# A float32 model kernel on one core: norm chain, convolution and expert routing reordered, and the tiles that a matmul holds placed 64 bytes off the tiles it streams

## What is computed

```
h = x * rsqrt(mean(x*x) + 1e-6) * w_norm        # rmsnorm over 2048
proj = h @ w_in                                  # 2048 x (2048..8192)
...mix proj by head...                           # 16 heads of 128, or recurrence
x = x + mixed @ w_out
```

```
y = b;  for i in range(4): y = y + xpad[:, i:i+s] * w[i]
r = sigmoid(y @ wa + ba);  i = sigmoid(y @ wx + bx)
```

## Time and profile before

| | |
|---|---|
| time, median of 3 runs | 3451.39 us (3450.22 to 3453.89) |
| the profiled execution | 3451.02 us, of which the span from first to last instruction is 3449.3 us |
| mean granted TensorE clock | 0.989 of full speed |
| TensorE matmuls (PE) | busy 3354.9 us, 97% of the span |
| VectorE (DVE) | busy 2239.6 us |
| ScalarE (ACT) | busy 1609.1 us |
| HBM read | 565.45 MB, 165 GB/s over the span |

### The profile page before, as it was taken

How to read it: one execution, slowest core, us unless ns; L and a number is a source line. 1 busy time by engine, 2 the same in 40 slices (tenths; PEclk the granted TensorE clock), 3 DMA queues, 4 the chain that set the end, 5 groups by cost and what they waited for, 6 DMA issues and landing times.

```text
span 3449.3 us, 64243 instructions
## 1 busy us (share of the span) xinstructions
PE 3354.9 (97%) x26164; PEld 3169.4 (92%) x26164; DVE 2239.6 (65%) x3581; ACT 1609.1 (47%) x2065; POOL 6.8 (0%) x27
## 2 busy tenths in 40 slices
PE   7999999999999899999999999999999999999998
PEld 7999998999999889999998999998899889998786
DVE  6767665545454555555546898775577657789855
ACT  4444454666664544545534444334433443344444
POOL 0000000000000000000000000000000000000000
PEclk9999999999999999999999999999999999999999
DMA  4444444444444345454444454445544554445454
GB/s 173 147 146 158 146 159 147 156 149 150 154 158 169 137 141 175 147 183 147 157 173 147 172 183 169 172 169 188 194 172 171 183 195 172 171 172 180 173 204 150
DMA packets 98921, 570.02 MB, mean 165 GB/s; under 512 B 9408, under 2 KB 30272, under 8 KB 31296
## 3 DMA queue, kind: packets, MB, share of 16 engines
q1 hardware_dynamic: 98752, 567.58, 46.2%
HBM read 565.45 MB, written 2.10 MB: 165 GB/s over the span
## 4 chain that ended last, share of the span: by engine, by line
PE 92%; DVE 3%; ACT 2%; issue 1%; DMA 1%; DVEq 1%; ACTq 0%; POOL 0%; POOLq 0%; SPq 0%
PE bank L477 21%; PE bank L478 21%; PE bank L479 20%; PE bank L938 7%; PE bank L936 7%; PE bank L937 7%; PE bank L860 1%; PE bank L604 1%; DVE oT L1377 1%; PE bank L548 1%; PE bank L790 1%; PE bank L795 1%; PE bank L499 1%; ACT wh L969 1%; PE bank L784 1%
## 5 line engine op out<-in xcount | busy, mean ns | idle before, releaser
L477 PE MATMUL bank<-hh,wh 128*128 128x256 f32 x5760 | 1661.6, 288 | 32.8 <-DVE hl L1382 27.9
L1362 DVE TENSOR_TENSOR wl<-raw,wh 128x1024 fp32r<-128x1024 f32 x1052 | 1254.1, 1221 | 604.0 <-ACT wh L969 597.5
L478 PE MATMUL bank<-hl,wh 128*128 128x256 f32 x5760 | 1627.5, 283 | 0.0
L479 PE MATMUL bank<-hh,wl 128*128 128x256 f32 x5760 | 1626.2, 282 | 0.0
L969 ACT ACTIVATE wh<-raw 128x1024 fp32r<-128x1024 f32 x1052 | 1051.1, 1049 | 339.0 <-DMA raw<-w_in_a 139.1
L477 PEld LDWEIGHTS bank<-hh,wh 128*128 128x128 f32 x5760 | 1108.0, 192 | 46.4 <-issue 37.1
L478 PEld LDWEIGHTS bank<-hl,wh 128*128 128x128 f32 x5760 | 1094.0, 190 | 8.2 <-issue 7.2
L479 PEld LDWEIGHTS bank<-hh,wl 128*128 128x128 f32 x5760 | 1088.3, 189 | 0.0
L936 PE MATMUL bank<-wh,ah 128*128 128x512 f32 x1024 | 402.1, 393 | 3.5 <-DVE al L1919 3.5
L938 PE MATMUL bank<-wl,ah 128*128 128x512 f32 x1024 | 401.9, 392 | 0.0
L937 PE MATMUL bank<-wh,al 128*128 128x512 f32 x1024 | 400.1, 391 | 0.0
(11 more groups left out here) (314 smaller groups left out, 2628.7 us busy)
## 6 DMA issues: line engine op xcount, KB each, us to landing
raw<-peer_u SPq DMA_DIRECT2D x128, 1024.0 KB, 4.8
raw<-peer_v SPq DMA_DIRECT2D x128, 1024.0 KB, 4.8
raw<-w_in_a SPq DMA_DIRECT2D x64, 1024.0 KB, 4.8
raw<-w_in_c SPq DMA_DIRECT2D x64, 1024.0 KB, 4.8
raw<-w_kv SPq DMA_DIRECT2D x32, 1024.0 KB, 4.8
raw<-w_in_b SPq DMA_DIRECT2D x32, 1024.0 KB, 4.8
raw<-w_out_a SPq DMA_DIRECT2D x16, 1024.0 KB, 4.8
raw<-w_out_b SPq DMA_DIRECT2D x16, 1024.0 KB, 4.9
```

The lines of the kernel that those rows point to most:

```text
L477: eng.matmul(out, h_[:, k, :], high[:, k, :], start=(k == 0), stop=False)
L478: eng.matmul(out, h_[:, k, :], low[:, k, :], start=False, stop=False)
L479: last = eng.matmul(out, low_rows(c, k), high[:, k, :], start=False, stop=(k == KC - 1))
L1362: eng.tensor_tensor(low_half_out(c, half), raw_half(c, half), high_half(c, half).bitcast(F32), ALU.subtract).then_inc(lo_ready, 1)
```

## The change

Five parts.

1. **Norm chain.** The last two out-projection columns are added and squared one by one, so that most is done before the last unit ends. A dummy `Sqrt` on a spare tile is put ahead, and `rstd` is made by one `Sqrt` and a VectorE reciprocal over 128x256. VectorE multiplies the norm weights into `oT` beforehand; the scaling is then one 128x512 product by `rstd` per pair. All eight scalings come first, then all eight low parts. ScalarE's copies for unit 2 of the next stage move behind the norm. The first two units of a stage are multiplied together (`two_products`): first all that needs only `hh`, four matmuls per chunk, then all that needs `hl`, two per chunk. At the kernel's start the norm is put ahead of the parameter arithmetic and the weight splits, and waits only for the constants that it uses; the first weight load comes in two halves.
2. **Convolution.** The low part of unit `u + 4` moves behind the convolution.
3. **Routing.** `ROUTE_UNITS` goes from 5 to 4; the softmax of both tiles is done together, its second half after the low part of U0's unit 29.
4. **Tail.** `Sqrt` and a 128x2 reciprocal in place of Ln and Exp, with the dummy `Sqrt` ahead; half of the last weighing moves into the wait.
5. **Placement.** `eps` and `qw` (4 bytes each, a row of 32) now stand ahead of `raw`, and `wh` directly behind `wl`. Byte addresses within a partition, and their rest by 128, of before and of the change:

The diff, cut to what the text speaks of:

```diff
-ROUTE_UNITS = 5
+ROUTE_UNITS = 4
...
+        eps = sb("eps", [P, 1])
+        qw = sb("qw", [P, 1])
         m = ExitStack()
         raw = sb_in(m, "raw", [P, RAW, KC * P])
         m.close()
         wl = sb("wl", [P, RAW, KC * P], F32R)
+        wh = [sb(f"wh{n}", [P, KC, P], F32R) for n in range(RAW)]
...
+            def two_products(c, outs, high, low, split):
+
+                for k in range(KC):
+                    if k % 2 == 0:
+                        eng.wait_ge(hh_ready, split + k // 2 + 1)
+                    for n in range(2):
+                        if k % FH == 0:
+                            eng.wait_ge(lo_ready, 2 * (c + n) + k // FH + 1)
+                        eng.matmul(outs[n], wh[(c + n) % RAW][:, k, :], high[:, k, :], start=(k == 0), stop=False)
+                        eng.matmul(outs[n], low_rows(c + n, k), high[:, k, :], start=False, stop=False)
+                for k in range(KC):
+                    if k % 2 == 0:
+                        eng.wait_ge(hl_ready, split + k // 2 + 1)
+                    for n in range(2):
+                        last = eng.matmul(outs[n], wh[(c + n) % RAW][:, k, :], low[:, k, :], start=False, stop=(k == KC - 1))
...
-            eng.wait_ge(consts_ready, 1)
+            eng.wait_ge(first_consts, 1)
             for g in range(KC // 2):
                 norm_sum("A", g)
...
+                eng.activation(spare[:, 0:1], eps[:, :], ACT.Sqrt)
                 eng.wait_ge(ss_done, 8 * (NORM_AT[name] + 1))
-                rsqrt(rstd[:, :], B[4][:, 0:T], 1.0 / D).then_inc(rstd_ready, 1)
+                eng.activation(rstd[:, :], B[4][:, 0:T], ACT.Sqrt, bias=eps[:, 0:1], scale=1.0 / D).then_inc(rstd_ready, 1)
...
+                eng.drain()
                 eng.wait_ge(rstd_ready, NORM_AT[name] + 1)
+                eng.reciprocal(rstd[:, :], rstd[:, :])
+                eng.drain()
+
+                def scale(n, g, weight):
+                    if n == 0:
+                        last = eng.tensor_tensor(oT[:, 2 * g:2 * g + 2, :], oT[:, 2 * g:2 * g + 2, :],
+                                                 rstd[:, :].unsqueeze(1).broadcast_to([P, 2, T]), ALU.mult)
...
+                    if n == 0 and name != "A":
+                        for g in range(KC // 2):
+                            scale(n, g, weight)
+                        for g in range(KC // 2):
+                            low(n, g, dst, high)
+                        low_part(0, NORM_UNIT[name] + 2)
...
                 low_part(i, u + 3)
-                low_part(i, u + 4)
                 eng.wait_ge(mm_done, unit(i, BASE["C"] + 1, 2, 2))
...
                 eng.drain().then_inc(s["xc_ready"], 1)
+                low_part(i, u + 4)
                 low_part(i, u + 5)
...
             for h in range(PEER_HEADS):
                 route(h)
-            for t in range(NT):
-                gates(t)
+            gate_distances()
             for c in range(ROUTE_FIRST + ROUTE_UNITS * PEER_HEADS, BASE["U1"]):
                 low_part(0, c)
-            eng.drain().then_inc(s["routed"], 1)
+                if c == BASE["U1"] - 3:
+                    gate_shares()
```

More of the change, by code:

```diff
@@ L841, in _ @@
             for g in range(PEER_HEADS):
[L842 to L846, removed]
+                if past_zero(g - 2):
+                    eng.wait_ge(s["qp_ready"], g - 2)
+                outs = [query_bank(g, j)[:, j * T:(j + 1) * T] for j in range(2)]
+                if g == 0:
+                    two_products(BASE["Q"], outs, hh, hl, SPLIT_AT["Q"])
+                else:
+                    for j in range(2):
+                        product(0, BASE["Q"] + 2 * g + j, outs[j], hh, hl)
                 if g >= 1:
@@ L1368, in low_part, with weigh_chunks @@
                 low_half(i, c, 1)
[L1370 to L1383 removed]
+            def weigh_chunks(weight, first, count):
+                for c in range(first, first + count):
+                    last = eng.tensor_scalar(oT[:, c, :], xT[:, c, :], col(weight, c), None, ALU.mult)
+                return last
@@ new lines, in stream_norm, with low @@
+            def stream_norm(name, outs, between=None):
+                eng.drain()
+                eng.wait_ge(rstd_ready, NORM_AT[name] + 1)
+                eng.reciprocal(rstd[:, :], rstd[:, :])
[4 more added lines that the diff above has]
+                                                 rstd[:, :].unsqueeze(1).broadcast_to([P, 2, T]), ALU.mult)
+                    else:
+                        for c in (2 * g, 2 * g + 1):
+                            last = eng.scalar_tensor_tensor(out=oT[:, c, :], in0=xT[:, c, :], scalar=col(weight, c),
+                                                            in1=rstd[:, :], op0=ALU.mult, op1=ALU.mult)
+                    last.then_inc(hf_ready, 1)
+                def low(n, g, dst, high):
+                    eng.wait_ge(hh_ready, SPLIT_AT[name] + 8 * n + g + 1)
+                    eng.tensor_tensor(chunk(dst, 2 * g, 2), chunk(oT, 2 * g, 2), chunk(high, 2 * g, 2).bitcast(F32),
+                                      ALU.subtract).then_inc(hl_ready, 1)
+                for n, (dst, high, weight) in enumerate(outs):
+                    if n == 0 and name != "A":
+                        for g in range(KC // 2):
[3 more added lines that the diff above has]
+                        low_part(0, NORM_UNIT[name] + 2)
+                    else:
+                        for g in range(KC // 2 + 1):
+                            if g < KC // 2:
+                                scale(n, g, weight)
+                            if between is not None:
+                                between(g)
+                            if g >= 1:
+                                low(n, g - 1, dst, high)
@@ L1454, in _ @@
             eng.tensor_scalar(rg_c[:, :], sp[:, 1, :], -RG_C, None, ALU.mult)
-            for c in range(3):
-                low_part(0, c)
-            stream_norm("A", [(hl, hh, "a_norm")])
             s = sA
@@ L2001, in _ @@
             eng.drain().then_inc(s["fss_ready"], 1)
+            weigh_stream(1, 1)
             eng.wait_ge(s["frs_ready"], 1)
+            eng.reciprocal(frstd[:, :], frstd[:, :])
+            eng.drain()
             for t in range(NT):
```

198 lines of the change are left out of this document (130 added, 68 removed).

## The result

The changed kernel takes 3392.07 us (median of 4, 3390.53 to 3395.45) against 3450.80 us (4 runs) of the kernel before: ratio 0.983, 95% interval 0.9813 to 0.9847, so 58.7 us less where 28.5 were forecast. The profiled execution took 3395.45 us, span 3393.7 us.

The account below looks back on a forecast made before the run. TensorE's own pace and its waits were taken to bound the kernel. The terms, with placement at 0, summed to -28.5 us: 3451.02 to 3422.5 us, own range 3412 to 3432, and 3408 to 3438 for 8 in 10.

Parts of the forecast that it names:

- Placement: 0: All matmuls: moving the tiles has no price either way, under 0.001 us a unit; bounded by a 260 us gain.
- placement speeds the matmuls: Rival, 5%: placement removes the unexplained 11 ns of small matmuls; all 260 us gives 3163, the page's pace 3217.
- Its second price: Rival that placement speeds matmuls, at the page's pace (109.2 ns a small matmul): 205 us less, 3217; rival's chance 5%.
- norms before C and Q: Norm chains ahead of stages C and Q: matmuls resume earlier, -5.0 us each, bounds 3 to 7 each.
- norm before F: Norm ahead of F, where VectorE makes a second output: -1.3 us, bounds 0 to 4.
- start: Kernel start, norm ahead of constants and table load: unit 1 starts at 35.7, was 39.27; -3.6 us, bounds 1.5 to 5.
- convolution: Gate matmuls behind the convolution: the moved low part no longer delays `xc`, -14.5 us, bounds 10 to 17.
- routing (U0): Four units a head: 7.9 us of VectorE stalls against 6.3 from early `routed`; +2.0 us, bounds -6 to +8.
- tail: Wait for `frstd` at the kernel's end: one table load goes, a small reciprocal comes; -1.1 us.
- M: Start of the last out-projection matmul before C, 1129.28 us; the prediction times the norm before C from it.
- the eighth wait: Convolution term: one wait put down to another releaser, counted like the seven gate-matmul stalls of 1.70 us each.
- the 6.3 us at `routed`: Routing term: early `routed` saves the 3.80 us wait, 0.28 of refill and some 2.3 of half clock.

Follow-up runs that it names:

- wh_0: The changed kernel with 192 bytes between `wl` and `wh`, so that `wh` lies 0 off `hh` and `hl` by 256 bytes: 3436.67 us, ratio 0.9959.
- place_undone: The changed kernel with `eps`, `qw` and `wh` allocated where they were, so that all addresses are those of before: 3419.65 us, ratio 0.9911.
- streams_128: The changed kernel with `kh`, `kl` and `ah`, `al` moved 128 bytes further on by pads: 3379.35 us.
- conv_back: The changed kernel with the low part of unit `u + 4` ahead of the convolution again: 3416.19 us, ratio 0.9892.
- place_alone: The kernel before with part 5 of the change (placement) and nothing else: 3427.88 us, ratio 0.9934.
- route_5: The changed kernel with five units per routing head, the softmax directly behind the heads and ScalarE's Exp two turns later: 3381.65 us, ratio 0.9794.

## Why the prediction was wrong

**The step that failed is "Placement: 0".** It inferred from two equal stretches that being 64 off has no price. The rows were read rightly; the inference assumed that each matmul has its own price, so that two in three and one in three would have to differ. The price is one of all the matmuls of a unit: with `wh` alone or `wl` alone at the right distance nothing happens (before, wh_0), with both the pace can be 113.3 ns. By that 43.8 us were gained at 256 columns and 13.1 lost in V, 30.7 net; 3.6 of it were lost again in U0 (below), and the changed kernel is 27.6 us faster than place_undone. The changed kernel was the first in which all three matmuls of a chunk were at that distance, and no stretch of before could have shown that.

The prediction's bound was mis-sized too: 0.02 us between the stretches allow 0.01 us a unit, some 4 us over the 365 units on `hh`, and not 0.001. It also reduced distances by 128, where 64 and 192 by 256 are different (streams_128), and it took `ah` for the streamed tile.

Of the rival "placement speeds the matmuls" the sign was right for 256 columns and its own size far off: 43.8 us of 212. Its second price came from a formula, N/2.4 + 2.5 ns, that the Trainium skill, TensorE: Matmul & The Clock Gate, "Back-to-back issue gap", gives for an isolated matmul, and not for a stream of them with a weight load each: 109.2 ns at 256 columns and 215.8 at 512. No stretch here is that fast: 113.3 and 226.7 ns are the least means seen. The Trainium skill, SBUF — State Buffer, "SBUF: two separate sides", says that TensorE never waits on anyone and lists a second read port for its weight loads. Here the placement of TensorE's own held and streamed tiles changes its pace, so this was no ground for a 0.

**The other terms**, from place_undone against the kernel before, both at 117.8 ns, in us:

| term | forecast | measured |
|---|---|---|
| norms before C and Q | -5.0, -5.0 | -4.8, -4.7 |
| norm before F | -1.3 | -1.6 (F's third unit) |
| start | -3.6 | -1.2 (third unit starts at 43.76, was 44.92) |
| convolution | -14.5 | -14.0 (stage C 467.0, was 481.0) |
| routing (U0) | +2.0 | +0.3 |
| tail | -1.1 | -1.3 |

These add up to -27.3. Two stretches that the sum didn't have give 3.1 more: the rest of stage X takes 82.4 us where it took 84.1, and the first two units of OC 11.4 where they took 12.8, where the granted clock was 0.88 in the kernel before and is 1.00 in place_undone. With them the sum is -30.4, and the two profiled executions differ by 30.0. So the 28.4 against 28.5 above is partly luck: the 2.4 us that the start fell short are made up by routing (1.7) and these two.

The first matmul came at M + 6.34 (forecast 6.5), the third unit at M + 20.3 (20.1), and the reciprocal, for which the rows of before had only 4 to 16 columns, took:

```profile
L1461 DVE RECIPROCAL rstd<-rstd x4: 1753/1753/1753, 16.6 to 1767.3; 128x256 f32<-128x256 f32 x4
```

1.75 us where 1.73 was extrapolated. The start is off because I ended its sum with the first unit. That unit's last chunks waited 1.9 us for the last `hl`, which VectorE made behind the two halves of the second unit's `wl`, so the second unit started at 36.7 and not at 35.7, and it then took 7.0 us where 5.65 is the full-clock time, part of it at half clock. In the convolution's sum the eighth wait was 1.0 us in the trace of before and not 1.70.

**The parts do not add.** Convolution and pace meet: VectorE's chain to `xc` has a fixed length, so at the faster pace the old order costs 20.5 us in stage C (conv_back) and not 14. Alone, the placement loses some 12 of its 32.7 us to such waits (place_alone). Routing went the other way: with four units a head VectorE is the bound in U0 whatever TensorE's pace, 192.43 us against 192.34 in place_undone, so the 3.6 us that the pace would give there are gone. Five units suit the changed kernel by 8.1 us; my forecast of 2 had the sign and not the size. It set against the stalls the 6.3 us at `routed` as if four units earned them. They come from the softmax done at once and the earlier `routed`: with five units that wait did not return either (route_5). The step from five units to four, with the softmax's second half behind most of the low parts, costs some 6 us even at the old pace (the estimate under route_5), and the +0.3 of the table is the sum of two larger effects.

## What to carry to other kernels

That two stretches take the same time shows only that those two states cost the same; a state in which all conditions hold at once needs its own run, and moving a tile by 64 bytes is the cheapest run there is. Try the distance of held and streamed tiles separately for each width of matmul, since what is best at 256 columns was among the worst at 512. When an engine becomes faster, reprice each wait of it for a chain of fixed length on another engine: there the gain is lost. And where two edits are priced in one term, as four units and the joint softmax were, try each without the other: the one can hide what the other costs.

## What the hardware showed

At full clock a matmul of 256 columns goes at 117.8 ns in the kernel before. With the streamed tile 192 bytes from both held ones by 256 it goes at one of two paces for a whole run, 113.3 or 117.8 ns; at the other distances the means were 117.8 to 119.9 ns. A run settles in its first few matmuls, and the pace then changes only where other matmuls, a wait or a change of clock come in between. One more matmul of some 25 ns there turned the 46 fast units of 96 to none, two more to all 96. The pattern of stage A differed between two profiles with the same code up to there. That this makes the spread of several us (3390.5 to 3395.5 here) fits, but is not shown: each kernel has one profile. What in the array or the memory sets the two paces was not measured; a conflict between the reading of the held and of the streamed tile would fit the dependence on placement by 256 bytes and on the moment, and is argued, not shown. At half clock the distance of starts is 213 ns, 256 columns at 1.2 GHz, with nothing on top, in the kernel before.
